# The first RMS norm's root moved behind the matmuls, and the selection of keys cut into parts

## The chip, the cores and the metric

The kernel runs on one core of a Trainium2 chip. The time is that of one execution on the device, in microseconds; of the kernel before, three runs gave 1718.41, 1720.13 and 1720.5 us, median 1720.13. The profile comes from an execution of its own, with a span of 1716.6 us from the first to the last instruction.

## The reference

Two blocks follow each other on x of 512 tokens by 1024 features. Only the first matters here:

```python
def rms_norm(x, g):
    xf = x.astype(jnp.float32)
    y = xf * lax.rsqrt(jnp.mean(xf * xf, axis=-1, keepdims=True) + EPS)
    return (y * g.astype(jnp.float32)).astype(x.dtype)

xn = rms_norm(h, norm_gain[layer])
proj = xn @ w_in[layer]
qa, ka, va, ga, qb, kb, vb, gb, iq, ik, iw, za, zb = jnp.split(proj, offsets, axis=-1)
ya = chunked_relpos_attention(qa, ka, va, rel_bias[layer]) * jax.nn.silu(ga)
# qb, kb, iq, ik get a partial rope; index scores are sum over heads of relu(iq . ik) * iw
# the 128 best keys of each query are selected (lax.top_k), and attended to by qb, kb, vb
yb = dsa_sparse_attention(qb, kb, vb, iq, ik, iw) * jax.nn.silu(gb)
gate_a = jax.nn.sigmoid(za + b_merge[layer, 0])
gate_b = jax.nn.sigmoid(zb + b_merge[layer, 1])
merged = gate_a * (ya @ w_branch_a[layer]) + gate_b * (yb @ w_branch_b[layer])
h = h + merged @ w_out[layer]
```

The root is one number per token (a factor of a whole row of xn). So it is a factor of each row of every projection too, and may be applied to x or to any of the products.

## The kernel before

The activations lie with features on the partitions: X is 8 tiles of 128 features by 512 tokens. All matrix products are in three passes: an operand is split into a high part (rounded to the format that TensorE multiplies at full rate, `fp32r`) and a low part (the rest), and high x high, low x high and high x low are summed in one PSUM bank. For X these parts are XH and XL, for weights WH and WL.

The weights come as a stream of slabs of 128 by 1024, which SyncE loads into a ring of four buffers RAW. ScalarE makes the high part of a slab (`high`, L1248, which reads RAW and writes WH), GpSimd the low part (`low`, L619, RAW less WH). WH and WL have two buffers each, so slab n+2 can be split only when the job on slab n is done. `split_past(name)` on ScalarE splits all slabs up to two beyond the job of that name; `evac(name, ...)` calls it, waits for the job and copies its bank out of PSUM.

A job is a projection of 128 features by 512 tokens: 8 tiles times 3 matmuls (L704 to L706), into one of the banks DB. The planner at the top (`plan_stream`) lists the jobs in the order of the stream, with the bank of each and the engine that empties it. The program of each engine is an order written out by hand, and semaphores join them. Around the change it is this:

- X is loaded by SyncE (even tiles) and ScalarE (odd tiles), then CONST and PAR, then four slabs.
- ScalarE squares the tiles (L1271), VectorE adds them (`add_square`, L1755), TensorE sums over partitions (`norm_sum`, L773), ScalarE takes the square root (L1282), VectorE inverts and broadcasts it (L1760, L1761), TensorE turns the result so that it stands on all partitions (`norm_spread`, L780).
- For each tile VectorE makes TMP = X x gain x root (L1783), ScalarE XH from it (L1289), VectorE XL = TMP less XH (L1787). TensorE's first job `vbiw` takes tile after tile as they come.
- TensorE goes on with `iq0`, turns of vb and iw, `iq1`, `ik`, `kb`, the rotations for rope (L850) of iq, `qa0`, the rotations of ik and kb, `qa1`. VectorE makes each rope in three instructions (L1806 to L1808) from tables COSI, SINI, COSB and SINB.
- The index scores follow: four small matmuls (L920), a job, four more, and so on. ScalarE applies the ReLU (L1398), VectorE adds head after head into MB (L1961, L1964).
- VectorE then selects keys: for each of three blocks of queries 16 rounds of `max` (L1975) and `match_replace` (L1976), 48 in all, with widths of 256, 384 and 512. TensorE meanwhile makes `va`, `qb`, `ga` and `gb`. The ropes of qb come behind the selection.
- Attention takes 32 pairs of steps: scores (L815), a minimum by row on VectorE (L1898), exponentials on ScalarE (L1348), scaling on VectorE (L1881), turns on TensorE (L842), a copy on ScalarE (L1358), products with v (L829). Tiles of the jobs `za0` to `za7` fill TensorE between them, two tiles in a step. ScalarE evacuates za in `next_bias`.
- For eight rounds the job `zb` and the packed job `pab` follow (L727 to L729), and VectorE gates and adds their outputs (L1989 to L1996).

Of the kernel before, what the change touches and what calls it, by code (L numbers as in the profile page):

```python
# [15 lines left out]
P = 128  # L16
# [54 lines left out]
def plan_stream():  # L71
# [21 lines left out]
    for k in range(4):  # L93
        add(f"qa{k}", 1, 1, KD, "act")
    for k in range(4):
        add(f"ka{k}", 1, 1, KD, "act")
# [110 lines left out]
XTB = XLB  # L207
# [17 lines left out]
def build(nc, stream, xt_in, memt_in, pars, convp, consts, rope_tabs, toep, masks8, resets, cz_in, pos_in, out):  # L225
    with ExitStack() as ctx:
# [65 lines left out]
        ROOTM = at("ROOTM", [P, MEM], A0 + 64)  # L292
        ROOT2 = at("ROOT2", [P, TOK], A0 + 18)
# [96 lines left out]
        consts_in = sem("consts_in")  # L390
        tabs_in = sem("tabs_in")
# [29 lines left out]
        xt_done = sem("xt_done")  # L421
# [167 lines left out]
        @block.sync  # L589
        def _(sp):  # L590

            for k in range(0, KD, 2):
                sp.dma_start(X[:, k, :], xt_in[k]).then_inc(x_in[k], 16)
            sp.dma_start(CONST[:, :, :], consts).then_inc(consts_in, 16)
            for j in range(RING):
# [78 lines left out]
        def _(pe):  # L674
# [257 lines left out]
            pe.wait_ge(irelu_done, n)  # L932
            pe.wait_ge(*emptied("va"))
# [303 lines left out]
        def _(act):  # L1237
# [46 lines left out]
            def norm_high(ni, n=TOK, halves=None):  # L1284

                for l, base in halves or ((0, XTB[ni]),):
                    for k in range(KD):
                        act.wait_ge(xt_done, base + k + 1)
                        A(XH[:, k, n * l:n * l + n], TMP[:, k % 2, 0:n], ACT.Copy).then_inc(xh_done, 1)  # L1289

# [10 lines left out]

            def norm_rest(ni):
                norm_std(ni)
                norm_high(ni)
# [59 lines left out]

            for k in range(1, KD, 2):
                act.dma_start(X[:, k, :], xt_in[k]).then_inc(x_in[k], 16)
            act.dma_start(PAR[:, :], pars).then_inc(consts_in, 16)
# [6 lines left out]
            act.wait_ge(consts_in, 16 * 2)  # L1374
# [4 lines left out]
            job_ready("vbiw")  # L1379
            A(SQ[0:72, 1, :], DB[JOBS["vbiw"].bank()][0:72, :], ACT.Copy).then_inc(act_emptied, 1)  # L1380
            evac("iq0", IQ[:, 0, :])
# [7 lines left out]
            evac("qa0", QA[:, 0, :], scale=DH ** -0.5)  # L1389
            evac("qa1", QA[:, 1, :], scale=DH ** -0.5)  # L1390
            n = 0
            for i in range(1, NT):
                w = P * (i + 1)
                for h in range(IDXH):
                    act.wait_ge(ilog_done, n + 1)
                    if n >= 4:
                        act.wait_ge(iacc_done, n - 3)
                    A(RELU[n % 4][:, 0:w], LOGIT[n % 4][:, 0:w], ACT.Relu).then_inc(irelu_done, 1)  # L1398
                    n += 1
                    if n in (4, 8):  # L1400
                        evac(f"qa{n // 4 + 1}", QA[:, n // 4 + 1, :], scale=DH ** -0.5)
                    elif n % 4 == 0:
                        evac(f"ka{n // 4 - 3}", KA[:, n // 4 - 3, :])
# [4 lines left out]
            for t in range(NT):  # L1408
                evac("va", VA[:, t, :], t=t)
            for k in range(4):  # L1410
                evac(f"qb{k}", QB[:, k, :], scale=DH ** -0.5)
            for k in range(4):
                evac(f"ga{k}", GA[:, k, :], ACT.Silu)
            for k in range(4):
                evac(f"gb{k}", GB[:, k, :], ACT.Silu)
            def next_bias(s):

                done, at_ = divmod(s["g"] // 2 - 4, 4)
                if s is segments["ab"][s["g"] // 2][0] and at_ == 0 and done >= 0:
                    evac(f"za{done}", ZA[:, done, :], ACT.Identity, bias=col("bm0", done))  # L1420
# [4 lines left out]
            evac("za7", ZA[:, 7, :], ACT.Identity, bias=col("bm0", 7))  # L1425
# [4 lines left out]
            for k in range(KD):  # L1430
# [4 lines left out]
                evac(f"zb{k}", SQ[:, k % 2, :], ACT.Sigmoid, bias=col("bm1", k))  # L1435
# [303 lines left out]
        def _(dve):  # L1739
# [25 lines left out]
            def norm(ni, srcs, halfway=None):  # L1765

                n = srcs[0][0].shape[-1]
                if ni == 0:
                    for k in range(1, KD):
                        add_square(ni, k, n)  # L1770

                    dve.wait_ge(consts_in, 16 * 2)
                dve.wait_ge(std_done, ni + 1)
                norm_root(ni, n)
                base = XTB[ni]
                for a in range(len(srcs) + 1):
                    if a == KD and halfway is not None:
                        halfway()
                    if a < len(srcs):
                        src, gain, _ = srcs[a]  # L1780
                        if base + a >= 2:
                            dve.wait_ge(xl_done, base + a - 1)
                        V.scalar_tensor_tensor(TMP[:, a % 2, 0:n], src, gain, SC[1][:, 0:n], ALU.mult, ALU.mult).then_inc(xt_done, 1)  # L1783
                    if a:
                        src, _, (k, c) = srcs[a - 1]
                        dve.wait_ge(xh_done, base + a)
                        V.tensor_tensor(XL[:, k, c], TMP[:, (a - 1) % 2, 0:n], XH[:, k, c].bitcast(F32),  # L1787
                                        ALU.subtract).then_inc(xl_done, 1)

            def x_norm(ni, gain):  # L1790
                norm(ni, [(X[:, k, :], col(gain, k), (k, slice(0, TOK))) for k in range(KD)])
# [77 lines left out]
            def attention(seg, beside=None, keep=False):  # L1869
# [13 lines left out]
                for k in range(n + 4):  # L1883
# [4 lines left out]
                    if k < n:  # L1888
# [12 lines left out]
                        if "rq" in s:  # L1901
                            dve.wait_ge(score_read, s["g"] + 1 - SCALED0)
                            least = ST[:, s["g"] % 4 - 1:s["g"] % 4 + 1]
                            V.scalar_tensor_tensor(least, least, -1.0, s["both"], ALU.mult, ALU.mult).then_inc(bm_done, 2)
                    if k >= 4:
# [18 lines left out]
            x_norm(0, "norm_gain")  # L1924
# [8 lines left out]
            V.tensor_tensor(LBC[:, 12:18], lg[2], mx, ALU.subtract).then_inc(lb_e, 1)  # L1933
            dve.wait_ge(lb_e, 2)
# [16 lines left out]
            rope(3, KBT[:, :], COSB[:, :], SINB[:, :])  # L1951

            n, off = 0, 0
            for i in range(1, NT):
                w = P * (i + 1)
                sc = MB[:, off:off + w]
                for h in range(IDXH):
# [7 lines left out]
                    n += 1  # L1965
                off += w
            dve.wait_ge(iacc_done, n)
            off = 0
            for i in range(1, NT):
                w = P * (i + 1)  # L1970
                sc = MB[:, off:off + w]

                link(V.memset(MB[0:CHUNK, off + w - CHUNK:off + w], BARRED))
                for _ in range(TOPK // 8):
                    link(V.max(MX8[:, :], sc))  # L1975
                    link(V.match_replace(sc, MX8[:, :], sc, TAKEN))  # L1976

                link(V.tensor_scalar(sc, sc, 0.5 * (TAKEN + BARRED), NEG, ALU.is_gt, ALU.mult))
                off += w
            for k in range(4):  # L1980
                rope(4 + k, QB[:, k, :], COSB[:, :], SINB[:, :])
            attention(segments["ab"])

            dve.wait_ge(o_out, 8)
            for k in range(KD):
                j = JOBS[f"pab{k}"]
# [561 lines left out]
```

## Time and profile before

| | |
|---|---|
| median of three runs | 1720.13 us (1718.41 to 1720.5) |
| the profiled execution, its own time | 1718.68 us |
| its span, granted clock | 1716.6 us, 0.997 |
| TensorE busy | 1678.4 us, 98% |
| VectorE busy | 870.3 us, 51% |
| ScalarE busy | 775.3 us, 45% |
| GpSimd busy | 702.4 us, 41% |

An engine's share is an average over stages. A busy TensorE is not one at its peak, since matmuls are pipelined and their ends are modelled: in a dense stretch one starts every 0.23 us, and each shows 0.39 us. Idle time of an engine other than the one that sets the end costs nothing by itself. Releasers are inferred.

### The profile page before, as it was taken

The numbers are of one execution on the slowest core, as the hardware profiler recorded it, in microseconds if no ns is written. First come the engines' busy times: TensorE is split into PE (matmuls) and PEld (weight loads), VectorE is DVE, ScalarE is ACT, GpSimd is POOL, SyncE is SP. The second block draws the span as 40 slices with busy tenths as digits, with TensorE's granted clock in tenths as the row PEclk, the third lists the DMA queues.
The fourth block names the chain that finished last, engine by engine and source line by source line (L and its number), as shares of the span: only waits on it lengthen the run. The fifth ranks groups of instructions, "written<-read, shape, count | busy, mean of one in ns | idle before, by whom it ended". The sixth has DMA issues, their size and how long they took to land.

```text
span 1716.6 us, 24469 instructions
## 1 busy us (share of the span) xinstructions
PE 1678.4 (98%) x8403; PEld 1362.7 (79%) x8403; DVE 870.3 (51%) x1678; ACT 775.3 (45%) x1194; POOL 702.4 (41%) x363
## 2 busy tenths in 40 slices
PE   6999999999999999999999999999999999999999
PEld 4778766787887889888888888888867888888887
DVE  4579466457634367846555541152464465555100
ACT  4333455435535454445544442335565554444222
POOL 2344311343544366534444444444301444444445
PEclk9999999999999999999999999999999999999999
DMA  5232211233332211123333333333201233322333
GB/s 194 86 111 86 87 50 38 86 99 99 113 108 86 87 50 38 38 76 97 98 98 98 93 93 108 110 104 86 74 14 27 96 98 98 98 94 92 108 102 118
DMA packets 43419, 151.71 MB, mean 88 GB/s; under 512 B 4944, under 2 KB 5072, under 8 KB 43344
## 3 DMA queue, kind: packets, MB, share of 16 engines
q1 hardware_dynamic: 41328, 145.62, 27.0%
q10 hardware_dynamic: 2016, 5.07, 0.9%
q8 instruction: 49, 0.80, 0.2%
q14 instruction: 26, 0.21, 0.0%
HBM read 148.58 MB, written 2.10 MB: 88 GB/s over the span
## 4 chain that ended last, share of the span: by engine, by line
issue 47%; PE 26%; POOL 23%; DVE 2%; POOLq 1%; DMA 1%; ACT 0%; SPq 0%; DVEq 0%
POOL WL L619 22%; PE DB L704 4%; PE DB L705 4%; PE DB L706 4%; PE SC L1005 2%; PE SC L815 2%; PE DB L842 1%; PE DB L754 1%; PE DB L756 1%; PE DB L755 1%; PE OB L829 1%; PE TB L704 1%; PE DB L829 1%; DMA RAW<-in_stream_dram 1%; PE OB L1035 0%
## 5 line engine op out<-in xcount | busy, mean ns | idle before, releaser
L619 POOL TENSOR_TENSOR WL<-RAW,WH 128x1024 fp32r<-128x1024 f32 x267 | 641.2, 2402 | 971.4 <-ACT WH L1248 971.4
L1248 ACT ACTIVATE WH<-RAW 128x1024 fp32r<-128x1024 f32 x267 | 282.9, 1060 | 638.5 <-PE DB L706 209.1
L1125 PE MATMUL DB<-XH,WL 128*128 128x512 f32 x640 | 249.0, 389 | 0.0
L1124 PE MATMUL DB<-XL,WH 128*128 128x512 f32 x640 | 249.0, 389 | 0.0
L1123 PE MATMUL DB<-XH,WH 128*128 128x512 f32 x640 | 249.0, 389 | 0.0
L704 PE MATMUL DB<-XH,WH 128*128 128x512 f32 x576 | 235.9, 410 | 6.2 <-DVE XL L1787 3.2
L706 PE MATMUL DB<-XH,WL 128*128 128x512 f32 x576 | 225.6, 392 | 0.0
L705 PE MATMUL DB<-XL,WH 128*128 128x512 f32 x576 | 225.5, 391 | 0.0
L704 PEld LDWEIGHTS DB<-XH,WH 128*128 128x128 f32 x576 | 108.7, 189 | 42.0 <-issue 16.3
L1123 PEld LDWEIGHTS DB<-XH,WH 128*128 128x128 f32 x640 | 120.1, 188 | 25.3
L1125 PEld LDWEIGHTS DB<-XH,WL 128*128 128x128 f32 x640 | 120.1, 188 | 25.0
L1124 PEld LDWEIGHTS DB<-XL,WH 128*128 128x128 f32 x640 | 120.1, 188 | 24.8
L1142 PE MATMUL DB<-GH,WH 128*128 128x512 f32 x352 | 136.9, 389 | 0.0
L1143 PE MATMUL DB<-GL,WH 128*128 128x512 f32 x352 | 136.9, 389 | 0.0
L1144 PE MATMUL DB<-GH,WL 128*128 128x512 f32 x352 | 136.9, 389 | 0.0
L706 PEld LDWEIGHTS DB<-XH,WL 128*128 128x128 f32 x576 | 108.7, 189 | 23.5
L705 PEld LDWEIGHTS DB<-XL,WH 128*128 128x128 f32 x576 | 109.0, 189 | 20.9 <-issue 1.4
L2250 DVE TENSOR_TENSOR DB<-DB,SQ 128x512 f32<-128x512 f32 x88 | 61.2, 695 | 40.9 <-PE DB L1125 40.1
L1143 PEld LDWEIGHTS DB<-GL,WH 128*128 128x128 f32 x352 | 66.1, 188 | 13.8
L1144 PEld LDWEIGHTS DB<-GH,WL 128*128 128x128 f32 x352 | 66.1, 188 | 13.7
L1142 PEld LDWEIGHTS DB<-GH,WH 128*128 128x128 f32 x352 | 66.1, 188 | 13.6
L2255 DVE SCALAR_TENSOR_TENSOR SB<-DB,CW,SB 128x511 f32<-128x511 f32 x44 | 33.0, 750 | 74.6 <-ACT SB L1626 74.6
(502 smaller groups left out, 2874.5 us busy)
## 6 DMA issues: line engine op xcount, KB each, us to landing
RAW<-in_stream_dram SPq DMA_DIRECT2D x268, 512.0 KB, 3.5
TP<-in_toep_dram ACTq DMA_DIRECT2D x4, 512.0 KB, 3.7
out_dram<-X SPq DMA_DIRECT2D x8, 256.0 KB, 4.3
X<-in_xt_dram SPq DMA_DIRECT2D x4, 256.0 KB, 5.2
X<-in_xt_dram ACTq DMA_DIRECT2D x4, 256.0 KB, 5.6
MRAW<-in_memt_dram ACTq DMA_DIRECT2D x2, 512.0 KB, 4.6
CONST<-in_consts_dram SPq DMA_DIRECT2D x1, 448.0 KB, 7.5
MSKI<-in_masks_dram ACTq DMA_DIRECT2D x1, 288.0 KB, 3.0
```

Of the source, the lines that this page charges most:

```text
L619: nc.gpsimd.tensor_tensor(WL[:, s, :], RAW[:, j, :], WH[:, s, :].bitcast(F32), ALU.subtract).then_inc(lo_done, 1)
L704: mm(o, WH[:, s, c], hi(k), start=(k == 0), stop=False)
L705: mm(o, WH[:, s, c], lo(k), start=False, stop=False)
L706: last = mm(o, WL[:, s, c], hi(k), start=False, stop=(k == job.kts - 1))
L1123: mm(o, WH[:, s, c], xh(k), start=(k == 0), stop=False)
L1124: mm(o, WH[:, s, c], xl(k), start=False, stop=False)
L1125: last = mm(o, WL[:, s, c], xh(k), start=False, stop=(k == KD - 1))
L1142: mm(o, WH[:, s, c], GH[:, k, :], start=(k == 0), stop=False)
L1143: mm(o, WH[:, s, c], GL[:, k, :], start=False, stop=False)
L1144: last = mm(o, WL[:, s, c], GH[:, k, :], start=False, stop=(k == FF - 1))
L1248: A(WH[:, n % SPLIT, :], RAW[:, n % RING, :], ACT.Copy).then_inc(hi_done, 1)
L2250: V.tensor_tensor(DB[j], DB[j], SQ[:, 0, :], ALU.mult).then_inc(scaled, 1)
```

## The change

The root of the first norm no longer goes into x. XH is X x gain, made by ScalarE as tiles arrive, and XL is made by VectorE in one instruction from X and XH. Slab 0 is loaded ahead of X, slab 1 ahead of X6, the parameters ahead of ScalarE's tiles. Squares and adds come behind the split. The root is spread behind `iq1` and kept as ROOT0. It enters where the products leave PSUM: in the rope tables (for iq, ik, kb, qb), in the scales of the columns for iw, vb and va, in the evacuation of qa and ka (now VectorE's, with the product), and for ga, gb, za and zb in a product within the bank before ScalarE reads it. TensorE multiplies zeros five times at the start. The selection of keys becomes a generator: 40 of 48 rounds first, the others between the gates' products.

```diff
+            sp.dma_start(RAW[:, 0, :], stream[0]).then_inc(raw_in[0], 16)
             for k in range(0, KD, 2):
                 sp.dma_start(X[:, k, :], xt_in[k]).then_inc(x_in[k], 16)
+                if k == 4:
+                    sp.dma_start(RAW[:, 1, :], stream[1]).then_inc(raw_in[1], 16)
...
-            pe.wait_ge(consts_in, 16 * 2)
-            norm_sum(0)
-            norm_spread(0)
+            pe.wait_ge(zeros_set, 1)
+            for _ in range(5):
+                mm(OB[:, :], PT[:, 0, 0:P], PT[:, 0, :], start=True, stop=True)
             feature_job("vbiw", xh, xl, xready=0)
             feature_job("iq0", xh, xl)
+            pe.wait_ge(consts_in, 16)
+            norm_sum(0)
...
-            for k in ("iq1", "ik", "kb"):
-                feature_job(k, xh, xl)
-            pe.wait_ge(tabs_in, 16 * 6)
+            feature_job("iq1", xh, xl)
+            norm_spread(0)
+            feature_job("ik", xh, xl)
             pe.wait_ge(vb_turned, 2)
             rotate(0, ROTI, IQ[:, 0, :], emptied("iq0"))
             rotate(1, ROTI, IQ[:, 1, :], emptied("iq1"))
+            feature_job("kb", xh, xl)
             feature_job("qa0", xh, xl)
...
+            act.dma_start(PAR[:, :], pars).then_inc(pars_in, 16)
             for k in range(1, KD, 2):
                 act.dma_start(X[:, k, :], xt_in[k]).then_inc(x_in[k], 16)
...
-            norm_squares(0, lambda k: X[:, k, :], lambda k: act.wait_ge(x_in[k], 16))
-            for n in range(SPLIT):
-                high(n)
+            high(0)
+            act.wait_ge(pars_in, 16)
+            for k in range(KD):
+                act.wait_ge(x_in[k], 16)
+                A(XH[:, k, :], X[:, k, :], ACT.Identity, scale=col("norm_gain", k)).then_inc(xh_done, 1)
+                if k == 4:
+                    high(1)
             split_next[0] = SPLIT
-            norm_rest(0)
+            norm_squares(0, lambda k: X[:, k, :], lambda k: None)
+            job_ready("vbiw")
+            act.wait_ge(acc_done, ACC[0] + KD - 1)
+            A(SQ[0:72, 1, :], DB[JOBS["vbiw"].bank()][0:72, :], ACT.Copy).then_inc(act_emptied, 1)
+            norm_std(0)
+            evac("iq0", IQ[:, 0, :])
...
-            A(IW[:, :, :], turned[:, :, DH:DH + IDXH], ACT.Copy, scale=float(IDXH ** -0.5 * IDXD ** -0.5))
-            A(VB[:, :, :], turned[:, :, 0:DH], ACT.Copy).then_inc(vb_turned, 1)
+            act.wait_ge(col_ready, 1)
+            for t in range(NT):
+                A(IW[:, t, :], turned[:, t, DH:DH + IDXH], ACT.Identity, scale=ST[:, 20 + t:21 + t])
+                last = A(VB[:, t, :], turned[:, t, 0:DH], ACT.Identity, scale=NR[:, t, :])
+            last.then_inc(vb_turned, 1)
...
+            def scaled_evac(name, *args, **kw):
+                split_past(name)
+                act.wait_ge(xscaled, SCALED.index(name) + 1)
+                evac(name, *args, **kw)
...
-                done, at_ = divmod(s["g"] // 2 - 4, 4)
+                done, at_ = divmod(s["g"] // 2 - 5, 4)
...
+            def first_scaled(name):
+                dve.wait_ge(slab_used, JOBS[name].done)
+                b = DB[JOBS[name].bank()]
+                V.tensor_tensor(b, b, ROOT0[:, :], ALU.mult).then_inc(xscaled, 1)
+
+            def first_out(name, dst, scale=1.0):
+                dve.wait_ge(slab_used, JOBS[name].done)
+                V.scalar_tensor_tensor(dst, DB[JOBS[name].bank()], scale, ROOT0[:, :], ALU.mult, ALU.mult).then_inc(dve_emptied, 1)
...
-            x_norm(0, "norm_gain")
+            V.memset(PT[:, 0, :], 0.0).then_inc(zeros_set, 1)
+            dve.wait_ge(pars_in, 16)
+            for k in range(KD):
+                dve.wait_ge(x_in[k], 16)
+                dve.wait_ge(xh_done, k + 1)
+                V.scalar_tensor_tensor(XL[:, k, :], X[:, k, :], col("norm_gain", k), XH[:, k, :].bitcast(F32), ALU.mult,
+                                       ALU.subtract).then_inc(xl_done, 1)
+            for k in range(1, KD):
+                add_square(0, k)
...
+            dve.wait_ge(std_done, 1)
+            norm_root(0)
+            link(V.tensor_copy(ROOT0[:, :], SC[1][:, :]))
+            V.tensor_scalar(ST[:, 20:24], NR[:, :, 0], float(IDXH ** -0.5 * IDXD ** -0.5), None, ALU.mult).then_inc(col_ready, 1)
...
+            for table in (COSI, SINI, COSB, SINB):
+                link(V.tensor_tensor(table[:, :], table[:, :], ROOT0[:, :], ALU.mult))
             rope(0, IQ[:, 0, :], COSI[:, :], SINI[:, :])
             rope(1, IQ[:, 1, :], COSI[:, :], SINI[:, :])
+            first_out("qa0", QA[:, 0, :], DH ** -0.5)
...
+            chosen = selection()
+            for _ in range(40):
+                next(chosen)
+            for k in range(8):
+                first_scaled(SCALED[k])
+                if 2 <= k < 6:
+                    rope(2 + k, QB[:, k - 2, :], COSB[:, :], SINB[:, :])
+                for _ in range(3 if k < 2 else KD if k == 6 else 0):
+                    next(chosen, None)
+
+            def gates_scaled(k):
+                if k and k % 4 == 0:
+                    first_scaled(f"za{k // 4 - 1}")
+
+            attention(segments["ab"], between=gates_scaled)
```

In attention `between(k)` is called behind the scores of pair k. Before each product of `pab{k}` VectorE calls `first_scaled(f"zb{k}")`.

## Rows read from the trace of the kernel before

**Rows 1.** By stage: us, busy PE, PEld, DVE, ACT, POOL (instructions), granted clock, DMA share, GB/s
```profile
0.00:18.80 18.80, 2.95 (x12) 2.49 (x12) 8.18 (x14) 9.73 (x15) 5.04 (x6) 1.00 0.92 340
18.80:34.40 15.60, 14.65 (x53) 10.15 (x53) 13.25 (x28) 6.82 (x11) 2.41 (x1) 1.00 0.18 60
34.40:58.03 23.63, 23.63 (x103) 18.83 (x102) 5.84 (x6) 6.48 (x10) 9.59 (x4) 1.00 0.33 109
```

**Rows 2.** Waits of TensorE, 0 to 60 us: total, times, longest
```profile
PE SC L773 <- DVE PB L1755: 11.6, 1, 11.6
PE DB L704 <- DVE XL L1787: 3.2, 3, 2.3
PE SC L780 <- DVE RS L1761: 2.0, 1, 2.0
```

**Rows 3.** Busy time by stage, 5 to 10 us, columns as in Rows 1
```profile
5.00:10.00 5.00, 0.00 (x0) 0.00 (x0) 3.46 (x5) 4.03 (x7) 0.00 (x0) 1.00 1.07 400
```

**Rows 4.** Timeline, 0 to 40 us: start, duration, engine, line, operands [idle before]
```profile
6.03 5.47 DVE L1755 TENSOR_TENSOR PB<-PB,SQ 128x512 f32<-128x512 f32 x7 [5.15 <-ACT SQ L1271]
...
11.62 1.06 ACT L1248 ACTIVATE WH<-RAW 128x1024 fp32r<-128x1024 f32 x1 [0.99 <-DMA RAW<-in_stream_dram]
...
12.90 1.06 ACT L1248 ACTIVATE WH<-RAW 128x1024 fp32r<-128x1024 f32 x1 [0.22 <-DMA RAW<-in_stream_dram]
...
16.60 1.41 DVE L1783 SCALAR_TENSOR_TENSOR TMP<-X,PAR,SC 128x512 f32<-128x512 f32 x2 [1.21 <-PE SC L780]
17.38 1.29 ACT L1289 ACTIVATE XH<-TMP 128x512 fp32r<-128x512 f32 x2 [3.27 <-DVE TMP L1783]
18.04 0.69 DVE L1787 TENSOR_TENSOR XL<-TMP,XH 128x512 fp32r<-128x512 f32 x1
18.77 0.75 DVE L1783 SCALAR_TENSOR_TENSOR TMP<-X,PAR,SC 128x512 f32<-128x512 f32 x1
...
20.77 0.63 PE L705 MATMUL DB<-XL,WH 128*128 128x512 f32 x1
...
28.89 1.06 ACT L1248 ACTIVATE WH<-RAW 128x1024 fp32r<-128x1024 f32 x1
...
30.03 2.41 POOL L619 TENSOR_TENSOR WL<-RAW,WH 128x1024 fp32r<-128x1024 f32 x1 [12.44 <-ACT WH L1248]
...
34.37 0.48 PE L704 MATMUL DB<-XH,WH 128*128 128x512 f32 x1
```

**Rows 5.** Instructions of L773 and L780: duration min/median/max in ns, first and last start
```profile
L773 PE MATMUL SC<-CONST,TMP x8: 250/250/250, 458.3 to 459.1; 128*128 128x1 f32 x8
...
L780 PE MATMUL OB<-CONST,TMP x4: 272/272/273, 482.5 to 482.8; 128*128 128x128 f32 x4
```

**Rows 6.** Timeline of TensorE: the two pairs of rotations
```profile
50.82 1.02 PE L850 MATMUL TB<-IQ,CONST 128*128 128x512 f32 x2
...
58.03 1.02 PE L850 MATMUL TB<-IK,CONST 128*128 128x512 f32 x2
```

**Rows 7.** Timeline of GpSimd, then of VectorE, 52 to 58 us
```profile
52.16 2.40 POOL L619 TENSOR_TENSOR WL<-RAW,WH 128x1024 fp32r<-128x1024 f32 x1 [3.04 <-ACT WH L1248]
...
52.67 2.42 DVE L1807 TENSOR_TENSOR IQ<-IQ,COSI 128x512 f32<-128x512 f32 x1
...
56.65 0.69 DVE L1807 TENSOR_TENSOR IQ<-IQ,COSI 128x512 f32<-128x512 f32 x1
```

**Rows 8.** Timeline of VectorE and of ScalarE: the 41st round, and the split behind `ga0`
```profile
155.69 0.69 DVE L1975 MAX8 MX<-MB 128x8 f32<-128x512 f32 x1
...
155.89 1.06 ACT L1248 ACTIVATE WH<-RAW 128x1024 fp32r<-128x1024 f32 x1 [3.90 <-PE DB L706]
```

**Rows 9.** Timeline of attention: probabilities scaled, and their turns
```profile
267.69 0.75 DVE L1881 TENSOR_SCALAR PB<-PB,ST 128x384 f32<-128x384 f32 x2
...
270.12 0.88 PE L842 MATMUL DB<-CONST,PB 128*128 128x128 f32 x6
```

**Rows 10.** Timeline of VectorE: a product of a `pab` job
```profile
350.35 0.69 DVE L1989 TENSOR_TENSOR TMP<-DB,ZA 128x512 f32<-128x512 f32 x1 [5.15 <-PE DB L729]
```

More of the change, by code:

```diff
@@ L204, in rooted @@
     return q - (q > 5)
-XTB = XLB
+SCALED = [f"{g}{k}" for g in ("ga", "gb", "za", "zb") for k in range(KD if g[0] == "z" else 4)]
 SPREAD_AT = [(4, 4), (5, 4), (5, 6)]
@@ L292, in build @@
         ROOTM = at("ROOTM", [P, MEM], A0 + 64)
+        ROOT0 = at("ROOT0", [P, TOK], A0 + 88)
         ROOT2 = at("ROOT2", [P, TOK], A0 + 18)
@@ L390, in build @@
         consts_in = sem("consts_in")
+        pars_in = sem("pars_in")
+        zeros_set = sem("zeros_set")
+        col_ready = sem("col_ready")
+        xscaled = sem("xscaled")
         tabs_in = sem("tabs_in")
@@ L590, in _ @@
         def _(sp):
+            sp.dma_start(RAW[:, 0, :], stream[0]).then_inc(raw_in[0], 16)
             for k in range(0, KD, 2):
                 sp.dma_start(X[:, k, :], xt_in[k]).then_inc(x_in[k], 16)
+                if k == 4:
+                    sp.dma_start(RAW[:, 1, :], stream[1]).then_inc(raw_in[1], 16)
             sp.dma_start(CONST[:, :, :], consts).then_inc(consts_in, 16)
-            for j in range(RING):
+            for j in range(2, RING):
                 sp.dma_start(RAW[:, j, :], stream[j]).then_inc(raw_in[j], 16)
@@ L932, in _ @@
             pe.wait_ge(irelu_done, n)
+            pe.wait_ge(*emptied("ka3", dve_emptied))
             pe.wait_ge(*emptied("va"))
@@ L1282, in norm_std @@
                 A(NR[:, 0:n // P, 0], SC[0][:, 0:n // P], ACT.Sqrt, scale=1.0 / D, bias=col("eps")).then_inc(std_done, 1)
[L1284 to L1289, printed above, removed]
             def late_tile(k, dk, b, gain, final=None):
@@ L1388, in _ @@
             evac("kb", KBT[:, :])
-            evac("qa0", QA[:, 0, :], scale=DH ** -0.5)
-            evac("qa1", QA[:, 1, :], scale=DH ** -0.5)
+            split_past("qa0")
+            split_past("qa1")
             n = 0
@@ L1400, in _ @@
                     if n in (4, 8):
-                        evac(f"qa{n // 4 + 1}", QA[:, n // 4 + 1, :], scale=DH ** -0.5)
+                        split_past(f"qa{n // 4 + 1}")
                     elif n % 4 == 0:
-                        evac(f"ka{n // 4 - 3}", KA[:, n // 4 - 3, :])
+                        split_past(f"ka{n // 4 - 3}")
             act.wait_ge(roped, 4)
@@ L1424, in _ @@
             attention(segments["ab"], next_bias)
-            evac("za7", ZA[:, 7, :], ACT.Identity, bias=col("bm0", 7))
+            scaled_evac("za7", ZA[:, 7, :], ACT.Identity, bias=col("bm0", 7))
             act.wait_ge(act_emptied, EMPTIED[JOBS["za7"].banks[0]][1])
@@ L1434, in _ @@
                     act.wait_ge(zb_used, k - 1)
-                evac(f"zb{k}", SQ[:, k % 2, :], ACT.Sigmoid, bias=col("bm1", k))
+                scaled_evac(f"zb{k}", SQ[:, k % 2, :], ACT.Sigmoid, bias=col("bm1", k))
                 split_past(f"pab{k}")
@@ L1763, in norm_root @@
                 dve.wait_ge(rs_spread, rooted(ni) + 1)
[L1765 to L1791, printed above, removed]
+            def first_scaled(name):
[5 more added lines that the diff above has]
+                V.scalar_tensor_tensor(dst, DB[JOBS[name].bank()], scale, ROOT0[:, :], ALU.mult, ALU.mult).then_inc(dve_emptied, 1)
             def split_out(hi, lo, src, signal=None):
@@ L1867, in group_out, with attention @@
                     dve.wait_ge(o_out, s["group"] + 1)
-            def attention(seg, beside=None, keep=False):
+            def attention(seg, beside=None, keep=False, between=None):
                 n, leaving = len(seg), []
@@ L1904, in attention @@
                             V.scalar_tensor_tensor(least, least, -1.0, s["both"], ALU.mult, ALU.mult).then_inc(bm_done, 2)
+                    if between is not None and k <= n:
+                        between(k)
                     if k >= 4:
@@ L1947, in _ @@
             dve.wait_ge(tabs_in, 16 * 6)
+            for table in (COSI, SINI, COSB, SINB):
+                link(V.tensor_tensor(table[:, :], table[:, :], ROOT0[:, :], ALU.mult))
             rope(0, IQ[:, 0, :], COSI[:, :], SINI[:, :])
             rope(1, IQ[:, 1, :], COSI[:, :], SINI[:, :])
+            first_out("qa0", QA[:, 0, :], DH ** -0.5)
             rope(2, IK[:, :], COSI[:, :], SINI[:, :])
             rope(3, KBT[:, :], COSB[:, :], SINB[:, :])
+            first_out("qa1", QA[:, 1, :], DH ** -0.5)
             n, off = 0, 0
@@ L1965, in _, with selection @@
                     n += 1
+                    if n in (4, 8):
+                        first_out(f"qa{n // 4 + 1}", QA[:, n // 4 + 1, :], DH ** -0.5)
+                    elif n % 4 == 0:
+                        first_out(f"ka{n // 4 - 3}", KA[:, n // 4 - 3, :])
                 off += w
             dve.wait_ge(iacc_done, n)
[L1968 to L1982, printed above, removed]
+            def selection():
+                off = 0
+                for i in range(1, NT):
+                    w = P * (i + 1)
+                    sc = MB[:, off:off + w]
+                    link(V.memset(MB[0:CHUNK, off + w - CHUNK:off + w], BARRED))
+                    for _ in range(TOPK // 8):
+                        link(V.max(MX8[:, :], sc))
+                        link(V.match_replace(sc, MX8[:, :], sc, TAKEN))
+                        yield
+                    link(V.tensor_scalar(sc, sc, 0.5 * (TAKEN + BARRED), NEG, ALU.is_gt, ALU.mult))
+                    off += w
+            chosen = selection()
[11 more added lines that the diff above has]
+            attention(segments["ab"], between=gates_scaled)
             dve.wait_ge(o_out, 8)
             for k in range(KD):
+                first_scaled(f"zb{k}")
                 j = JOBS[f"pab{k}"]
```

21 lines of the change are left out of this document (6 added, 15 removed).

## Prediction

> **What bounds the kernel now.** I read the page first: TensorE is busy 98% of the span, so a gain can only come from time in which TensorE has nothing to do or works at half pace. The table of stages says where that is: up to 18.80 us it is busy 2.95 us in 12 instructions, from 18.80 to 34.40 it still loses a little, and from 34.40 on it is full [rows 1]. The waits name the causes: 11.6 us for the last sum of squares, 2.0 us for the broadcast root, 3.2 us for low parts XL [rows 2]. The timeline gives the order: seven adds end at 11.5, then sum, root, spread, and only at 16.60 the first scaled tile. One tile then takes 0.75 + 0.69 us of VectorE with 0.63 us of ScalarE between them, and the first slab's job follows at that pace. Its end is seen in the split of slab 2 (28.89), which waits for it; `iq0` follows, and `iq1` begins at 34.37 [rows 4]. The landmark used below is that start of `iq1`, and behind it the end of `qa0` (58.03, where the second pair of rotations begins [rows 6]). Behind those TensorE waits for little.
>
> **The change, part by part.** All times are a clock from the span's start.
>
> Arrival. With 400 GB/s moved from 5 us on [rows 3] and slab 0 used in the old order at 11.62, when some 3.0 MB had been asked for ahead of and with it (eight X tiles 2.0, CONST 0.45, PAR 0.06, slab 0 0.5), a transfer lands at about 4.1 us + 2.5 us per MB asked for before it on both queues; slab 1, 0.5 MB on, was used at 12.90, which agrees. New order: slab 0 lands at 6.0, X0 near 7.2, X2 8.8, X4 near 9.8, slab 1 near 11.1. Estimates, good to 1 us.
>
> Split of x. ScalarE: slab 0 high part (1.06 us) to 7.1; X0 to X4, each 0.63 us or its arrival, to 10.7; slab 1's high part 11.1 to 12.2; X5 to X7 to 14.1. The low part of a slab on GpSimd is 2.41 us [rows 4]. VectorE now makes XL in one instruction from two SBUF operands (X and XH). I price it at 0.69 to 0.75 us, as the two old ones.
>
> Here is the catch. A VectorE multiply with both operands in SBUF takes 0.69 us when GpSimd is idle and 2.42 us when it starts while GpSimd makes a low part: 52.67 + 2.42 = 55.09, just half a microsecond past GpSimd's end at 54.56 [rows 7]. So I take it that such an instruction waits for GpSimd's to end. Slab 0's low part holds XL0 until 9.5, XL0 is ready at 10.2; slab 1's low part asks at 12.2, gets in behind XL3, and holds the rest for 2.4 us: XL7 is ready at 17.5. TensorE ends `vbiw` one tile later, 18.2 (28.7 before). If nothing were held, XL7 would come at 13.7 and `vbiw` end at 14.6; if slab 1 landed 1 us later, at 19. The Trainium skill says the same of the ports ("SBUF — State Buffer", section "SBUF: two separate sides"): VectorE, in an instruction with two SBUF inputs, and GpSimd take a shared pair of ports exclusively and for a whole instruction. The trace agrees, with 2.42 against 0.69 us; without it `iq1` would start 3 us sooner (rival A). It speaks against this change, which puts eight such instructions beside two low parts, where the old ones stood behind them.
>
> Slab 1 and `iq0`. `iq0` takes 5.45 us at full rate (34.37 to 50.82 is three jobs), so it ends at 23.7. Slab 2 is the next bound: ScalarE makes its high part behind the eight squares. The adds start behind XL7 and take 5.47 us for seven, so end at 23.0; the last square ends 0.9 us sooner, slab 2's high part is at 23.2 and its low part at 25.6. TensorE meanwhile makes the sum (0.9 us: 458.3 to 459.1 plus one [rows 5]) and the four turns, ready at 25.3. So `iq1` starts at 25.7 instead of 34.37: 8.7 us gained. The five zero matmuls lie in idle time before 10 us. They should save the half pace (0.63 us for the matmul at 20.77 against 0.48 for the one at 34.37 [rows 4], granted clock 1.00 in both stretches [rows 1]), but those first tiles are paced by XL, so I give them nothing; at the 1.2 GHz level throughout the first four tiles they would cost under 0.5.
>
> `iq1` to `qa0`. The same four jobs and rotations, plus the spread (four turns, 0.7 us [rows 5]), now inside the full stream. Cost 0.7, so the gain at the end of `qa0` is 8.0. What could be late: from `iq1`'s end E, spread to E+0.7, ROOT0 copied and the column made by E+1.7, eight small ScalarE copies to E+3.0 (0.15 to 0.2 us each), only then slab 4's high and low part, E+6.5. TensorE wants it at E+7.5 (`ik` and two rotations first). Cover 1 us. ScalarE's queue behind that wait is what decides here: `evac("iq1")`, the split of slab 4, and `ik`. On VectorE: 11 small instructions, four table products (0.69 each, up to 2.4 more for each of the low parts they meet), two ropes; done near E+17 where TensorE asks at E+19. Cover 2 us. Both ends for this part: 0 and 4 us lost; I take 0, nearest to rows 6 with nothing waiting there.
>
> Banks emptied by VectorE (`qa`, `ka`, 8 x 0.75 us). Each stands in the gap between a job's end and the ReLUs, where VectorE waits 2.4 us or more; ScalarE gets 0.58 us back. Nothing.
>
> Selection in parts. The 40th round ended before `ga0` was done: the 41st starts at 155.69, ScalarE's split behind `ga0` at 155.89 [rows 8]. With one `first_out` more in front it ends 0.5 us late, and the evacuation of `ga0` with it, in ScalarE's queue only. Three rounds (4.5 us) fit in a job of 5.45. The rotations of qb and the selection of all parts are done before attention, as before. Cost 0 to 1, taken 0.1.
>
> Roots at 24 banks (0.69 us each, 16.6 us of VectorE in all). Gates ga, gb: above. Eight za in attention: VectorE puts it behind the scores of every fourth pair. The tightest place: probabilities scaled from 267.69 to 268.4 are turned by TensorE at 270.12 [rows 9], 1.7 us of cover, and the insertion comes behind them; the next pair has over 3. za's evacuation moves one pair later on ScalarE, where it sat idle 2 us. Nothing. Eight zb: VectorE is idle 5.15 us per round before the product [rows 10]; nothing. Bounds of the 24: 0 and all 16.6; taken 0.1.
>
> Sum: 8.7 − 0.7 − 0.2 = 7.8 us. The profiled execution had a span of 1716.6 and 1718.68 us in all; less 7.8 it is 1708.8 and 1710.9. The median of the three runs is 1720.13, 1.4 above that execution; from it: **1712.3 us**.
>
> **Rivals.**
> A. The holding doesn't bite in the head (GpSimd gets in later, or the tiles land sooner). For it: the estimates of arrival are mine, and XL and the low part may interleave kindly. Against: 2.42 us in every row of this kind. Then `vbiw` ends at 14.6, slab 2's low part at 22.7, gain 11.5 − 0.7 − 0.2: 1709.5.
> B. A new wait stands between `iq1` and the index scores: slab 4 behind the column of roots, or the tables and ropes behind GpSimd, 3 us past the covers of 1 and 2. For it: the chain has five engine changes. Against: the cover. 1715.3.
> C. The first part does not do what it says: slab 1 and X6 land 5 us later (small parameter rows first on their queue, and the transfers of both queues slow each other), or `iq1` is held by slab 2 alone. X tiles still gate XL. Gain 2: 1718.
> D. The other side. VectorE becomes the bound where its 24 root products stand. ScalarE waits for each before its evacuation and before the next exponentials; if those waits reach TensorE, 0.69 x 24 = 16.6 us less 7.8 gives +8.8: 1729. It decides from 12 exposed ones on (7.9 / 0.69). For it: TensorE and VectorE work in lockstep in attention. Against: covers of 1.7 us and 5.15 us.
>
> **How the numbers follow.** Forecast 0.52 (its own range 1710.5 to 1714), A 0.16, B 0.16, C 0.10, D 0.06. Likeliest: 1712.3. Eight in ten, with A, B and the start of C: 1708 to 1717.5. What this kernel's measurement can tell from no change is about 0.2%, 3.4 us: under 1716.7 is faster. Forecast, A and most of B lie there: faster 0.84. C mostly within, with some of B and D: same 0.10. D's rest: slower 0.06.
>
> **What would show it.** In the changed kernel `vbiw` should end near 18 with one XL of about 3 us beside slab 1's low part; `iq1` start near 26, held by GpSimd; no TensorE wait over 1 us from there to the first index scores; TensorE's stretch of attention as long as before. Wrong if the first job ends before 16 or after 21, if TensorE waits for slab 4 or a rope, or if the stretch from the end of `qa0` to the end of attention grows by over 1 us.

## The result, and the profile after

| | before | after |
|---|---|---|
| median, 14 runs each | 1715.71 us (1713.36 to 1721.58) | 1706.81 us (1704.74 to 1712.63) |
| ratio, 95% interval | | 0.995 (0.9938 to 0.9961) |
| the profiled execution, its own time | 1718.68 us | 1712.5 us |
| its span, granted clock | 1716.6 us, 0.997 | 1710.7 us, 0.994 |
| VectorE busy | 870.3 us | 895.0 us |

Faster by 6.7 to 10.6 us (the interval times 1715.7). The forecast was 1712.3 with a range of 1708.0 to 1717.5: right in direction, but the time lies 1.2 us under the range. The kernel before has its three early runs among the 14; all of them are above its median. One execution in all the experiments, of the kernel with the products doubled, was granted 0.553 of the clock and took 2802.84 us; its median below counts it, its ratio does not.

The head, in the timeline of the changed kernel: what is early is early by less waiting, and the order is the one forecast.

```profile
1.50 6.36 PE L898 MATMUL OB<-PT 128*128 128x512 f32 x10 [1.50 <-DVE PT L1921]
4.74 1.06 ACT L1259 ACTIVATE WH<-RAW 128x1024 fp32r<-128x1024 f32 x1
5.87 2.35 POOL L626 TENSOR_TENSOR WL<-RAW,WH 128x1024 fp32r<-128x1024 f32 x1 [5.42 <-ACT WH L1259]
6.88 4.54 DVE L1926 SCALAR_TENSOR_TENSOR XL<-X,PAR,XH 128x512 fp32r<-128x512 f32 x5 [5.44 <-ACT XH L1374]
8.92 0.47 PE L711 MATMUL DB<-XH,WH 128*128 128x512 f32 x1 [1.07 <-DVE XL L1926]
...
10.72 1.06 ACT L1259 ACTIVATE WH<-RAW 128x1024 fp32r<-128x1024 f32 x1 [1.23 <-DMA RAW<-in_stream_dram]
...
11.86 2.37 POOL L626 TENSOR_TENSOR WL<-RAW,WH 128x1024 fp32r<-128x1024 f32 x1 [3.63 <-ACT WH L1259]
...
12.50 3.60 DVE L1926 SCALAR_TENSOR_TENSOR XL<-X,PAR,XH 128x512 fp32r<-128x512 f32 x3 [1.07 <-ACT XH L1374]
...
14.84 0.50 PE L711 MATMUL DB<-XH,WH 128*128 128x512 f32 x1 [2.25 <-DVE XL L1926]
...
15.83 0.63 PE L711 MATMUL DB<-XH,WH 128*128 128x512 f32 x1
16.03 5.46 DVE L1767 TENSOR_TENSOR PB<-PB,SQ 128x512 f32<-128x512 f32 x7
...
21.59 2.40 POOL L626 TENSOR_TENSOR WL<-RAW,WH 128x1024 fp32r<-128x1024 f32 x1 [7.36 <-ACT WH L1259]
...
24.05 0.94 PE L780 MATMUL SC<-CONST,PB 128*128 128x1 f32 x8
...
25.10 0.47 PE L711 MATMUL DB<-XH,WH 128*128 128x512 f32 x1
```

It answers to [rows 4]. (The five multiplications of zeros are ten instructions in the first line.) Three XL instructions take 3.60 us instead of 2.2, because one of them stands beside slab 1's low part (11.86 to 14.23). TensorE pauses 2.25 us for it, and then works at half pace: 0.63 us for a matmul, the mark that [rows 4] showed at 20.77. `iq1` starts at 25.10 instead of 34.37, and nothing holds it: slab 2's low part has been ready since 23.99.

The waits of TensorE, 0 to 460 us of the changed kernel (in total, times, longest):

```profile
PE DB L711 <- DVE XL L1926: 3.3, 2, 2.3
PE DB L711 <- issue: 1.8, 3, 0.8
PE DB L711 <- ACT VA L1274: 1.7, 1, 1.7
PE OB L898 <- DVE PT L1921: 1.5, 1, 1.5
PE DB L836 <- ACT PT L1358: 0.6, 2, 0.4
PE DB L711 <- POOL WL L626: 0.3, 1, 0.3
```

The 11.6 and 2.0 us of [rows 2] are gone. The waits for VA and for PT are in the kernel before too (1.6 and 0.6 us), and so is the last line (0.3 us, at 428 us there, at 419 here). The same view of the kernel before has one more line that the changed kernel has not:

```profile
PE SC L920 <- DVE KBT L1808: 0.4, 1, 0.4
```

How the gain travels, by starts of the same work before and after: `iq1` 34.37 and 25.10 (9.3 us sooner), rotations of ik 58.03 and 49.25 (8.8), first index scores 65.76 and 56.55 (9.2), first attention scores 197.49 and 188.38 (9.1), first `pab` matmul 322.89 and 313.78 (9.1). The 0.5 us lost by 49.25 is the spread (four turns, 0.60 us, now in the full stream), and the 0.4 regained behind it is the wait for the rope of kb just shown. Attention is as long as before: 125.40 us in both.

But the two profiled spans differ by 5.9 us only. The windows show where 3.2 went. Busy time by stretch (us, PE, PEld, DVE, ACT, POOL, granted clock, DMA share, GB/s), first the kernel before, then the changed one:

```profile
440.00:480.00 40.00, 36.96 (x249) 34.27 (x248) 16.18 (x32) 19.16 (x28) 21.50 (x9) 0.96 0.42 130
...
600.00:650.00 50.00, 46.03 (x324) 40.84 (x324) 33.95 (x63) 23.53 (x44) 33.18 (x43) 0.97 0.17 53
...
1190.00:1240.00 50.00, 49.83 (x287) 43.33 (x286) 17.72 (x30) 25.42 (x42) 15.95 (x7) 0.97 0.24 74
```

```profile
440.00:480.00 40.00, 36.66 (x263) 34.57 (x261) 16.22 (x32) 16.07 (x25) 21.47 (x9) 0.96 0.43 132
...
600.00:650.00 50.00, 46.53 (x330) 42.51 (x328) 34.33 (x59) 23.84 (x40) 35.73 (x49) 0.97 0.11 34
...
1190.00:1240.00 50.00, 49.15 (x265) 41.42 (x264) 20.51 (x44) 26.65 (x49) 14.21 (x6) 0.90 0.23 72
```

In the last stretch the changed kernel's execution has 0.90 where the other has 0.97: 0.07 x 50 us = 3.5 us of TensorE's full pace missing. That is code which the change doesn't touch, and it varies from run to run: the profiled execution of the first experiment, the changed kernel once more, has 0.96, 0.97 and 0.97 there, as the kernel before, and its span is 1707.5 us, 9.1 under 1716.6. That is the gain of the landmarks. A kernel's times go with the mean granted clock of the run:

| granted clock | before, us | after, us |
|---|---|---|
| 0.998 | 1714.84 to 1715.42 | 1704.52 to 1704.92 |
| 0.997 | 1716.46 to 1716.91, four at 1718.5 to 1719.1 | 1705.75 to 1706.36, one at 1708.16 |
| 0.996 | 1718.06 to 1720.42 | 1707.02 to 1710.04 |
| 0.995 | 1721.28 to 1722.24 | 1710.28 to 1710.51 |
| 0.994 | 1723.39 to 1723.74 | 1712.50 to 1712.63 |

(After: its 20 runs, here and in the first experiment. Before: its runs beside the experiments, of which three more lie at 0.999 and 1.000, 1712.22 to 1713.75.) From 0.998 to 0.994 each kernel loses about 8. Line by line the medians differ by 10 to 12 us, but a line doesn't compare like with like. The half pace in the changed kernel's head counts in its clock (0.57 from 15 to 19 us, 0.97 over the first 60); the half pace in the old head does not ([rows 1] has 1.00 around the 0.63 us of [rows 4]). 0.03 x 60 us is 0.001 of the whole. Compared one line lower (0.998 before with 0.997 after, and so on), the medians differ by 8.6 to 9.6 us, which agrees with the 9.1.

### The profile page after: what moved, and what is told of

The parts are those of the page before. It is cut to its first block, busy times and chain, and to the rows that moved or that the text cites. A ratio compares the mean times of both kernels' runs of the same rounds, so it can differ in the third digit from the quotient of the medians.

```text
span 1710.7 us, 24552 instructions
## 1 busy us (share of the span) xinstructions
PE 1684.7 (98%) x8413; PEld 1366.9 (80%) x8413; DVE 895.0 (52%) x1709; ACT 773.4 (45%) x1192; POOL 702.7 (41%) x363
## 3 DMA queue, kind: packets, MB, share of 16 engines
q1 hardware_dynamic: 41328, 145.62, 27.3%
## 4 chain that ended last, share of the span: by engine, by line
issue 48%; PE 27%; POOL 23%; DVE 1%; POOLq 1%; DMA 0%; ACT 0%; SPq 0%; DVEq 0%; ACTq 0%
POOL WL L626 23%; PE DB L711 5%; PE DB L713 4%; PE DB L712 4%; PE SC L1016 2%; PE SC L822 2%; PE DB L849 1%; PE DB L761 1%; PE DB L763 1%; PE DB L762 1%; PE OB L836 1%; PE TB L711 1%; PE DB L836 1%; PE OB L1046 0%; DMA RAW<-in_stream_dram 0%
```

## The experiments

Ratios are to the kernel before, on the same chip and in the same session (its medians there 1716.58, 1716.91 and 1716.74 us); each kernel ran 5 to 12 times. "Attention" is the start of the first attention scores, 188.38 in the changed kernel and 197.49 before.

**The changed kernel again.** No edit.

> The changed kernel again, with the kernel before on the same chip, to settle the level that both are measured from. Theory (the forecast's step in time was right, its starting level wrong): the difference is 7 to 10 us, as 8.9 us of the two medians of 14 runs, and single runs of both kernels differ by the granted clock, by some 2 us for each 0.001 of it. Rival (the size of the step is off): a difference under 5 or over 12 us at equal clock.

Measured 1706.69 us (1704.52 to 1709.32), 0.994 [0.9927, 0.9953], 9.9 us under the kernel before beside it. The first measurement holds. The kernel before, at 1716.58, again stays under the 1720.13 from which I had started.

**The selection in one piece.**

```diff
-            for _ in range(40):
-                next(chosen)
+            for _ in chosen:
+                pass
```

> The selection of keys undone to one piece: all 48 rounds ahead of the first product with the root. Theory (parts are needed because the gates' banks now wait for VectorE): the product of ga0 comes some 12 us after its job, ScalarE stands in front of the split of ga3's slab, TensorE waits 5 to 7 us once for GpSimd; 5 to 7 us slower than the changed kernel. Rival (ScalarE and the two slabs in hand cover it, so the cut is worth nothing): within 1 us of the changed kernel.

Measured 1717.4 us, 0.9998 [0.9988, 1.0008]: the whole gain is gone, 10.7 us against the changed kernel, where I had expected 5 to 7. Its timeline behind `ga0`:

```profile
160.01 0.60 ACT L1274 ACTIVATE GA<-DB 128x512 f32<-128x512 f32 x1 [10.77 <-DVE DB L1781]
...
161.63 5.12 POOL L626 TENSOR_TENSOR WL<-RAW,WH 128x1024 fp32r<-128x1024 f32 x2 [11.21 <-ACT WH L1259]
...
164.12 0.76 PE L711 MATMUL DB<-XH,WH 128*128 128x512 f32 x1 [5.54 <-POOL WL L626]
164.68 0.63 PE L712 MATMUL DB<-XL,WH 128*128 128x512 f32 x1
```

This is one chain to be read upwards from the effect. TensorE stands 5.54 us for a low part, GpSimd stood 11.21 us for a high part, ScalarE stood 10.77 us for VectorE's product. An evacuation that waits for VectorE holds the splits behind it in ScalarE's queue. Then TensorE runs at half pace from 164.7 to 168.1. Attention starts at 196.28, 7.9 us later than in the changed kernel. The other 2.8 us lie behind it. In the profiled execution 2.0 of them are one low stretch: from 440 to 480 us it has 0.91 where the changed kernel has 0.96 (0.05 x 40 us). Whether the uncut selection brings that about is not shown; the run without the zeros has 0.91 there too, with the selection cut.

**The same cut in the kernel before.** Selection as a generator there too: 40 rounds, three behind each of `ga0` and `ga1`, the ropes of qb behind `ga2` to `gb1`, the rest behind `gb2`.

> The kernel before, with nothing changed but the selection of keys: 40 rounds of max and match_replace first, then three behind each of ga0 and ga1, the ropes of qb behind ga2 to gb1, the rest behind gb2, each of them once the job of that name is done. My theory: the cut is worth 10.7 us in the changed kernel only because there ScalarE's evacuation of ga0 waits for VectorE's product. Here nothing that ScalarE or TensorE does waits for the selection, so the ratio to the kernel before is 1.000 (0.998 to 1.002), and the first attention scores stand at 197.5 us, within 0.2. Rival: the selection as one piece costs time in the kernel before as well (its VectorE instructions hold up something else), and the cut alone makes it 3 us or more faster; then a part of the change's gain was the cut's own.

Measured 1718.29 us, 0.9998 [0.9984, 1.0013]; attention at 197.4. The cut by itself is worth nothing. It is a condition for the deferral as built here, not a part of the gain.

**The 24 root products doubled.**

```diff
                 V.tensor_tensor(b, b, ROOT0[:, :], ALU.mult).then_inc(xscaled, 1)
+                link(V.tensor_tensor(b, b, ROOT0[:, :], ALU.mult))   # ahead of it
```

> Each of the 24 products of a bank with the root is made twice, so ga, gb, za and zb carry the root squared (the only part of the computation that is changed); 16.6 us more on VectorE. Theory (these products are hidden): 0 to 1 us slower than the changed kernel. Rival (they stand on TensorE's path): 8 to 17 us slower, and the same products already take as much of the change's gain.

The root enters ga, gb, za and zb twice. Measured 1707.4 us, 0.9946 [0.9931, 0.996]; attention at 188.38, first `pab` matmul at 313.96, 0.2 us later than after. The last eight products stand behind that landmark; for them only the time speaks, less than 1 us above the changed kernel's on the same chip. Twice the products is hidden as well, and rival D is out.

**Without the zeros.** The five zero matmuls left out.

> Without the five matmuls of zeros. Theory (the first tiles are paced by XL and the pause before XL5, not by TensorE): within 0.5 us of the changed kernel or up to 1.4 us faster, since TensorE then has less of a pause at 12.3 us behind which it fell to half pace. Rival (they save the half pace): the first fifteen matmuls start 0.43 us apart and the kernel is some 3 us slower.

```profile
8.81 0.77 PE L711 MATMUL DB<-XH,WH 128*128 128x512 f32 x1 [8.81 <-DVE XL L1924]
9.38 0.63 PE L712 MATMUL DB<-XL,WH 128*128 128x512 f32 x1
...
14.84 0.50 PE L711 MATMUL DB<-XH,WH 128*128 128x512 f32 x1 [0.48 <-DVE XL L1924]
...
24.00 0.50 PE L711 MATMUL DB<-XH,WH 128*128 128x512 f32 x1 [0.26 <-POOL WL L626]
```

Measured 1707.44 us, 0.9947 [0.9933, 0.9961], the same as after. The first nine products now go at half pace, but they were paced by XL: all they do is to fill the pause before XL5, 0.48 us instead of 2.25. No slow stretch follows it, and `iq1` starts 1.1 us sooner (24.00). Attention follows (187.28), the time doesn't, within its interval. The zeros buy fast products where products are not what is waited for.

**Slab 1's high part behind all of XH,** and, in a second kernel, X6 loaded ahead of slab 1 too.

```diff
-                if k == 4:
-                    high(1)
+            high(1)
```

> Slab 1's high part is made behind XH7 instead of behind XH4, so its low part on GpSimd comes behind all XL; the loads stay as they are. Theory (XL5 is held 2.3 us by slab 1's low part): no XL is longer than 0.75 us in that stretch, the first job ends near 14 to 15 instead of 18.4, and iq1 starts near 24, some 1 us sooner; the low part holds an add of squares instead. Rival (X5 to X7 arrive late and pace the XL anyway): the first job still ends near 18, nothing gained.

> As the one before, and X6 is loaded ahead of slab 1. Theory (holding, then arrival): all XL by 12, the first job at full pace from 8.9 to 14.4, iq0 from 15, iq1 from 23, held by the squares, adds and slab 2 behind them; 2 us faster than the changed kernel. Rival (slab 1 arrives too late for iq0): no gain over the changed kernel.

Measured 1706.32 us, 0.9927 [0.9911, 0.9943], and 1708.25 us, 0.9937 [0.9914, 0.9961]. In both, slab 1's low part holds no XL; slab 0's still holds XL0 (the second kernel's, first line: 6.61 us for eight, of which XL0 1.97):

```profile
6.70 6.61 DVE L1924 SCALAR_TENSOR_TENSOR XL<-X,PAR,XH 128x512 fp32r<-128x512 f32 x8 [5.25 <-ACT XH L1373]
...
15.73 0.50 PE L710 MATMUL DB<-XH,WH 128*128 128x512 f32 x1 [1.22 <-POOL WL L625]
...
23.51 0.50 PE L710 MATMUL DB<-XH,WH 128*128 128x512 f32 x1 [0.93 <-POOL WL L625]
24.34 0.63 PE L710 MATMUL DB<-XH,WH 128*128 128x512 f32 x1
```

`iq1` starts 0.7 and 1.6 us sooner than in the changed kernel. But slabs 1 and 2 are now what TensorE waits for, and a half-pace stretch stands behind that (25.7 to 28.7, and 24.3 to 27.3). Attention starts at 189.36 and 188.42, 1.0 us and nothing later than after. The hold is real and worth nothing here: its removal only moves the pause. My 2 us for the second kernel missed.

**Slabs 0 and 1 loaded and split behind all X tiles.**

> Slabs 0 and 1 are loaded and split behind all of X, as in the kernel before, with the root still deferred. Theory (the gain is the deferral itself; the order of loads gives little): the first job starts near 14 with all XL ready and runs at full pace, iq1 near 26 to 27, 1 to 2 us slower than the changed kernel. Rival (the early slab carries the gain): 4 us or more slower.

```profile
12.13 1.99 ACT L1258 ACTIVATE WH<-RAW 128x1024 fp32r<-128x1024 f32 x2
...
13.25 5.14 POOL L625 TENSOR_TENSOR WL<-RAW,WH 128x1024 fp32r<-128x1024 f32 x2 [12.80 <-ACT WH L1258]
15.19 7.73 DVE L1765 TENSOR_TENSOR PB<-PB,SQ 128x512 f32<-128x512 f32 x7 [2.11 <-ACT SQ L1281]
15.67 0.80 PE L710 MATMUL DB<-XH,WH 128*128 128x512 f32 x1 [6.86 <-POOL WL L625]
```

Measured 1713.44 us, 0.9971 [0.9958, 0.9983]: 6.7 us slower than after. My 1 to 2 us missed, the rival was right. I had counted the 1.25 us of a transfer. What counts is that the first job needs the low part of its slab, 2.4 us of GpSimd behind 1 us of ScalarE behind the arrival. It starts at 15.67 instead of 8.92, at half pace again, and the adds take 7.73 us instead of 5.46, since the two low parts stand beside them. Attention starts at 193.43, 5.1 us later.

**The same early slabs in the kernel before.** Slab 0 loaded ahead of X and split ahead of the squares, slab 1 loaded ahead of X6.

> The kernel before, with nothing changed but the order of the loads and of two ScalarE instructions: slab 0 is loaded ahead of the X tiles and slab 1 ahead of X6; slab 0's high part is made ahead of the squares, slab 1's behind them. In the changed kernel this early order carried about 5 of the gained 9 us. My theory: it does so only because there the first job starts with the first tile; here the first job waits for the root anyway (first scaled tile at 16.60), so the order gives nothing, and costs what later X tiles, or adds held by the low part of slab 0 (2.4 us), cost the sum of squares: iq1 starts 0 to 3 us later than 34.37, ratio 1.000 to 1.0015. Rival: the order is worth something by itself, because the low parts of slabs 0 and 1 are out of the way when VectorE scales the tiles: iq1 starts 1 us or more sooner.

Measured 1721.22 us, 1.0012 [0.9996, 1.0028]; attention at 199.1, 1.6 us later than before. The adds take 6.48 us and end 2.5 us later, held by slab 0's low part (6.29 to 8.64) after later tiles:

```profile
6.29 2.35 POOL L622 TENSOR_TENSOR WL<-RAW,WH 128x1024 fp32r<-128x1024 f32 x1 [5.84 <-ACT WH L1251]
...
7.49 6.48 DVE L1758 TENSOR_TENSOR PB<-PB,SQ 128x512 f32<-128x512 f32 x7 [6.62 <-ACT SQ L1274]
```

So the order of loads that carries 5 to 7 us of the changed kernel's gain gives nothing alone (by the landmark a loss of 1.6 us, in the time none that is clear of 1.000). Neither part has a price of its own.

**An attempt to beat both.** X6 ahead of slab 1, slab 2 split behind the third square, `iq0` and `iq1` back to back with the sum behind them, the spread inside `ik`, `kb` ahead of the rotations, ScalarE empties three banks before it waits for the column of roots.

```diff
             feature_job("iq0", xh, xl)
+            feature_job("iq1", xh, xl)
...
-            feature_job("iq1", xh, xl)
-            norm_spread(0)
-            feature_job("ik", xh, xl)
+            for k, _ in enumerate(feature_tiles("ik", xh, xl)):
+                if k == 3:
+                    norm_spread(0)
+            feature_job("kb", xh, xl)
```

> A version that may beat both: X6 ahead of slab 1, slab 1 split behind XH7, slab 2 split behind the third square, TensorE goes straight from iq0 into iq1 and takes the sum behind it, the spread between tiles of ik, kb ahead of the rotations, and ScalarE evacuates iq0, iq1 and ik ahead of its wait for the column of roots. Theory (TensorE's stream from the first tile on is the bound, and its gaps were the holding of XL, slab 2 behind the squares and slab 4 behind the column): qa0 ends 3 to 4 us sooner than in the changed kernel and the time falls by as much. Rival (the ropes now come too late): the rotations of ik wait for them and at least half is lost again.

Measured 1707.29 us (1706.44 to 1710.54), 0.9935 [0.9917, 0.9953]. No half pace is left in the head. First index scores, attention (186.35) and `pab` (311.76) all come 2.0 us sooner than after, where I had expected 3 to 4: TensorE still pauses 1.65 us for XL7, which took 2.87 us beside slab 1's low part (12.54 to 14.92). The profiled executions of this and of the changed kernel have the same low stretches (0.96, 0.97 and 0.90), and their spans are 1708.7 and 1710.7 us: there the 2.0 us reach the end. The medians don't show it. Four of the five runs, at a granted clock of 0.996 to 0.997, stand at 1706.44 to 1708.35, among those of the changed kernel. What the head gives here is smaller than one run's share of low clock later on, so I cannot call it a win.

## Why the prediction was wrong, and where it was right

The step that failed is the last of the sum: "the median of the three runs is 1720.13, 1.4 above that execution; from it: 1712.3". The forecast was 5.5 us too high. 4.4 of it is this starting level (1720.13 against 1715.71 over 14 runs, the three among them); 1.1 is the gain (8.9 by medians against 7.8; by the landmarks 9.1). With the same gain from 1715.71 it would have been 1707.9. The size of the change was right: 7.8 lies within the measured 6.7 to 10.6. The profile could have warned of the level: its execution had three low stretches outside the change, and nothing said that the other runs have as many. The range was built from the costs of the change alone and had no term for the level.

By its steps:

- **Arrival.** Right to 1.3 us, not to the 1 that I gave: slab 0 was used at 4.74 (forecast 6.0), slab 1 at 10.72 (11.1).
- **Split of x.** Right in kind, both holds came: slab 0's low part ran 5.87 to 8.22 and held XL0, which was ready about 8.9, not 10.2. Slab 1's held one XL as forecast. `vbiw` ended at 18.4 (18.2), but for another reason: XL7 came at 16.1 and not at 17.5, and seven matmuls at 0.43 instead of 0.23 us apart (15.4 to 18.4) ate the difference.
- **Rival A** said the hold is worth 3 us. Taken away it gives 1.6 at `iq1` and nothing at attention; slabs 1 and 2 are next.
- **`iq1`** at 25.10, forecast 25.7. The bound was mis-named: slab 2 was ready at 23.99 (25.6 forecast), as the adds began at 16.03 (the last XL ended at 16.1, not at 17.5). TensorE's own stream, with the half pace in it, set the start. 9.3 gained, 8.7 forecast.
- **The stream.** Forecast loss 0.7 + 0.2, measured 0.2: the spread cost 0.5, and I had not looked for a wait of the old order that would go (0.4 us for the rope of kb).
- **Covers.** Slab 4's low part was ready at 37.64 (34.88 + 2.76) and its first matmul stood at 37.92, as close behind the rotations as in the kernel before (1.32 us behind the start of the pair). So it held nothing, but of the cover of 1 us 0.3 was left. Rival B did not happen, by little.
- **Selection.** "Cost 0 to 1, taken 0.1" is right for the cut. Its counterpart I never priced: left whole, it costs all of the gain. As an extra part of a change, it is what the rest stands on.
- **Roots at 24 banks.** Taken 0.1; doubled, they cost 0.2 by the landmark at `pab`. Right.
- **Zeros.** Taken 0; right in the time. Not foreseen: the pause they leave brings the half pace back, at 1.1 us of `iq1`.

## What to carry to other kernels

When a factor is moved behind the matmuls, look at every engine that must now apply it: an evacuation that waits for a product holds all that is queued behind it, and what that engine was busy with (here 48 rounds of selection) must be cut before the move pays. Price the parts of such a change together, since deferral, early slabs and the cut are worth 9 to 10 us together, and the early slabs and the cut nothing each alone. Take the starting level from as many runs as there are, at the granted clock that they show; three runs of a kernel whose runs reach from 1712 to 1724 us are no level.

## What the runs showed of the hardware

- A pause of TensorE can be paid twice. Behind 2.25 us came 3.0 us at 0.63 us a matmul (15.4 to 18.4); behind 5.54 us, 3.4; behind 0.93 us after an earlier one of 1.2 to 1.5, 3.0. The windows of the kernel with the selection in one piece show it as granted clock:

```profile
158.00:164.00 6.00, 0.58 (x2) 0.00 (x0) 5.87 (x8) 3.46 (x5) 2.37 (x2) 0.81 0.00 0
164.00:169.00 5.00, 4.88 (x13) 3.85 (x14) 3.27 (x2) 0.00 (x0) 2.75 (x1) 0.55 0.53 145
```

  A granted clock of 0.55 is the lower of the two levels (1.2 of 2.4 GHz) for most of the stretch. It is not so each time: in the attempt to beat both, 1.65 us ahead of 15.52 were followed by no half pace in the head, and without the zeros, 0.48 us by none either. What decides between these cases, and what makes the low stretches at 460 and 1210 us come and go, stays open.
- The hold between VectorE and GpSimd takes small instructions as well. In the changed kernel a product of 128 by 6 elements and the table products, beside a low part:

```profile
21.59 2.41 DVE L1935 TENSOR_TENSOR LBC<-LBC,PAR 128x6 f32<-128x6 f32 x1
...
34.71 0.69 DVE L1958 TENSOR_TENSOR SINI<-SINI,ROOT 128x512 f32<-128x512 f32 x1
34.88 2.76 POOL L626 TENSOR_TENSOR WL<-RAW,WH 128x1024 fp32r<-128x1024 f32 x1 [6.18 <-ACT WH L1259]
35.44 2.75 DVE L1958 TENSOR_TENSOR COSB<-COSB,ROOT 128x512 f32<-128x512 f32 x1
```

  It goes both ways: GpSimd's 2.40 us became 2.76 where it started beside a VectorE product. `max` and `match_replace`, 384 wide, stayed at 0.56 and 0.54 us beside the low part of 131.60 as without one. The Trainium skill ("SBUF — State Buffer", section "SBUF: two separate sides") has this as an exclusive lock between a VectorE instruction with two SBUF inputs and a GpSimd instruction that reads SBUF, held for the whole instruction by the one that starts first. These rows agree.
- One such hold makes the stretch at 620 us come and go. There VectorE multiplies QX, from two SBUF operands, while GpSimd makes subtractions without a gap (some 0.63 us each). In the changed kernel the product took 3.63 us, as long as five of them; in the kernel with the products doubled (last three lines) it took 0.73 us, and the subtraction beside it 1.08:

```profile
616.82 3.63 DVE L2177 TENSOR_TENSOR QX<-HKQ,SQ 128x512 f32<-128x512 f32 x1
...
622.71 1.45 PE L1021 MATMUL SC<-QX,KX 128*128 128x128 f32 x6 [2.73 <-DVE PT L2197]
```

```profile
616.72 0.73 DVE L2178 TENSOR_TENSOR QX<-HKQ,SQ 128x512 f32<-128x512 f32 x1
616.83 1.08 POOL L663 TENSOR_TENSOR SB<-HB 128x256 f32<-128x256 f32 x1
...
620.45 0.94 PE L1021 MATMUL SC<-QX,KX 128*128 128x128 f32 x6 [0.58 <-DVE PT L2198]
```

  Of the twelve profiled executions eight have the long form (3.62 to 3.64 us), and in these TensorE waits 2.7 to 3.0 us and the clock from 600 to 650 us is 0.97, once 0.93. Four have the short form (0.72 to 0.73 us), a wait of 0.6 us and a clock of 1.00. Code that no experiment touched is thus worth over 2 us in one run and not in the next: at a granted clock of 0.996, the profiled executions of two variants with the short form took 1707.04 us (products doubled) and 1707.56 us (X6 ahead of slab 1), those with the long form 1709.32 us (the changed kernel again) and 1709.74 us (without the zeros).
